# Samples' attention over the cache: two samples at a time, queries as weights, value products on 32-column strips

## The reference

```python
def _nsa_sel_attend(q, qpos, idx, kvb):
    ...
    s = jnp.einsum('btgrd,btgkld->btgrkl', q, kb) * dh ** -0.5
    kpos = idx[..., None] * NSA_BLOCK + jnp.arange(NSA_BLOCK)
    mask = kpos <= qpos[None, :, None, None, None]
    p = _masked_softmax(s.reshape(B, T, G, R, -1), mask.reshape(B, T, G, 1, -1))
    return jnp.einsum('btgrn,btgnd->btgrd', p, vb.reshape(B, T, G, -1, dh).astype(jnp.float32))
...
    o = gt[..., 0:1] * o_c + gt[..., 1:2] * o_s + gt[..., 2:3] * o_w
```

## Time and profile before

| | us |
|---|---|
| median of 3 runs | 4247.26 (4228.52 to 4252.52) |
| the profiled execution, its own time | 4233.27 |
| its span in the trace | 4231.4 |
| mean granted clock of PE, share of full speed | 0.897 |
| the samples' units, from about 1880 to 2396 in the span | 516 |

### The profile page before, as it was taken

The page is one execution under the profiler, slowest core; times in us unless marked ns, Lnnn a source line. Parts: engine busy times, 40 slices in busy tenths (PEclk is TensorE's granted clock), DMA queues, the critical chain, the costliest instruction groups (busy, mean ns, idle before and its releaser), DMA issues. The chain is left out here.

```text
span 4231.4 us, 44095 instructions
## 1 busy us (share of the span) xinstructions
PE 3769.7 (89%) x17890; PEld 2507.1 (59%) x17890; DVE 1431.0 (34%) x3327; ACT 546.9 (13%) x1219; POOL 181.7 (4%) x279
## 2 busy tenths in 40 slices
PE   7998989999999999869888457676879999999998
PEld 4665666665677776658776443333446556665676
DVE  3445322233132232265564346542242213211111
ACT  1000011000111001111121024441011000100000
POOL 3111100000000000000000000000000000000000
PEclk8999999999999999866666658888999999999999
DMA  6565542322343323351221320004003333233443
GB/s 162 172 189 162 171 120 81 86 61 85 115 118 88 98 82 108 105 111 48 72 92 65 73 85 8 6 3 157 15 10 116 89 96 112 74 90 95 138 122 96
DMA packets 601110, 399.64 MB, mean 94 GB/s; under 512 B 90140, under 2 KB 577933, under 8 KB 596429
## 3 DMA queue, kind: packets, MB, share of 16 engines
q1 hardware_dynamic: 573084, 312.00, 27.1%
q0 software_dynamic: 13824, 67.12, 4.6%
q10 hardware_dynamic: 14000, 17.71, 1.2%
HBM read 364.80 MB, written 36.13 MB: 95 GB/s over the span
## 5 line engine op out<-in xcount | busy, mean ns | idle before, releaser
L400 PE MATMUL psum<-arena 128*128 128x384 f32 (+1 forms) x4224 | 1338.0, 475 | 24.3 <-DVE arena L535 15.8
L400 PEld LDWEIGHTS psum<-arena 128*128 128x128 f32 x4224 | 799.8, 192 | 493.2 <-issue 32.3
L410 PE MATMUL psum<-arena 128*128 128x384 f32 (+1 forms) x2112 | 662.1, 472 | 0.0
L410 PEld LDWEIGHTS psum<-arena 128*128 128x128 f32 x2112 | 399.9, 191 | 235.4 <-issue 4.8
L433 PE MATMUL psum<-arena 128*128 128x384 f32 (+3 forms) x816 | 271.4, 489 | 0.0
L549 DVE SCALAR_TENSOR_TENSOR arena<-arena,psum 128x384 f32<-128x384 f32 (+1 forms) x132 | 70.3, 532 | 582.0 <-ACT arena L487 581.8
L487 ACT ACTIVATE arena<-psum 128x384 f32<-128x384 f32 (+1 forms) x132 | 62.5, 473 | 1356.6 <-PE psum L400 1356.6
L565 DVE SCALAR_TENSOR_TENSOR arena<-psum,arena 128x384 f32<-128x384 f32 (+1 forms) x96 | 51.4, 536 | 506.6 <-PE psum L410 506.6
L558 DVE TENSOR_TENSOR arena<-psum,arena 128x384 f32<-128x384 f32 (+1 forms) x132 | 70.7, 536 | 423.0 <-PE psum L400 422.1
L433 PEld LDWEIGHTS psum<-arena 128*128 128x128 f32 (+1 forms) x816 | 153.2, 192 | 96.3 <-issue 19.5
L3406 PE MATMUL psum<-arena 128*128 128x128 f32 x528 | 87.6, 318 | 86.5 <-DVE arena L3503 54.1
(11 more groups left out here) (582 smaller groups left out, 3655.0 us busy)
## 6 DMA issues: line engine op xcount, KB each, us to landing
arena<-in_ffa_up SPq DMA_DIRECT2D x132, 512.0 KB, 5.2
arena<-in_ffb_up SPq DMA_DIRECT2D x132, 512.0 KB, 5.2
arena<-in_ffa_down SPq DMA_DIRECT2D x48, 704.0 KB, 4.5
arena<-in_ffb_down SPq DMA_DIRECT2D x48, 704.0 KB, 4.5
arena<-in_w_in SPq DMA_DIRECT2D x27, 1024.0 KB, 5.8
arena<-in_w_in SPq DMA_DIRECT2D x9, 1056.0 KB, 6.0
pT<-arena ACTq DMA_DIRECT2D x32, 192.0 KB, 5.3
arena<-xs SPq DMA_DIRECT2D x2, 2176.0 KB, 14.9
```

The source lines that it names most:

```text
L400: ins = mm(b[:, 0:n], w[:, g, k], hC[:, k, 0:n], start=(k == 0), stop=(k == KD - 1))
L410: ins = mm(b[:, 0:n], w[:, k], actT[:, k, 0:n], start=(k == 0), stop=(k == FH - 1))
```

## The change

Two samples are worked on together: sample 2u+x lies on partitions 64x to 64x+63 of everything that has queries on partitions. There are 4 pairs u, each with 4 page units c = 0 to 3 (one page of 1024 rows from each sample) and the window unit c = 4, 20 units v in all, one every 2 rounds: 46 rounds instead of 53.

- Scores: the 64 query columns are now the weights and 512 turned keys the moving side; two samples write to column strips 0 to 63 and 64 to 127 of one bank. A page unit has two such pairs (`scores(v, 0)`, `scores(v, 1)`), a window unit one. Scores lie with queries on partitions and cached rows along the free side.
- DVE adds the mask, scales and takes the running minimum in one instruction (`tensor_tensor_reduce`, in `masked`), ACT's exponential has that minimum as bias and gives the sum (`accum_out`). The turns of the maximum, the spreading and the matmul of sums go away. The exponentials of a pair's four page units are brought to one maximum at its end.
- The weights must be turned (`turn_weights`, 8 for a page unit) and copied by ACT (`weights`) before the value products.
- Value products: one for each sample, tile of 128 rows and group: 32 weight columns, 64 value columns, written to strip 64x+32g. There are 576 of these where there were 288 of 64 by 128.
- The window rows go to free places of `sVB`, loaded by SP when a unit is done. Gathers for unit v+3 start when unit v's values of the same x are read. The compressed branch is laid out by pairs as well. 16 small loads of gate biases move to ACT's queue.

The core of the diff (left out: the layout of tiles, the small loads, the masks' preparation, and the finish of a pair, `6 in stage` and `7 in stage`, with about 15 small DVE operations for each u):

```diff
         SA_FIRST = 10
-        SA_UNITS = sorted([(SA_FIRST + 6 * q + 3 * h, 0, q, h) for q in range(NB) for h in range(2)] +
-                          [(SA_FIRST + 6 * q + 1, 1, q, 0) for q in range(NB)])
-        SA_ROUNDS = SA_FIRST + 6 * NB - 3 + 8
+        SA_UNITS = [(u, c) for u in range(4) for c in range(5)]
+        SA_ROUNDS = SA_FIRST + 2 * len(SA_UNITS) + 6
 
         def sa_active(r):
 
-            return [(br, q, h, r - start) for start, br, q, h in SA_UNITS if 0 <= r - start <= (5 if br else 6 + h)]
+            units = [(v, r - SA_FIRST - 2 * v) for v in range(len(SA_UNITS))]
+            return [(v, s) for v, s in units if 0 <= s <= (7 if SA_UNITS[v][1] == 4 else 5)]
...
@@ sa_pe
+            def keys(v, x):
+                u, c = SA_UNITS[v]
+                if c == 4:
+                    pe.wait_ge(cache_in[x], 16 * (u + 1))
+                else:
+                    pe.wait_ge(sa_pages[sa_slot(v, x)], sa_gathered(v, x))
+                for half in range(1 if c == 4 else 2):
+                    b = bank(rt)
+                    for t in range(4):
+                        ins = turn(b[:, t * P:(t + 1) * P], sVB[sa_slot(v, x)][:, 4 * half + t, 0:P], ident)
+                    ins.then_inc(rt.full, 1)
+                turned[v] = rt.n
+
+            def scores(v, half):
+                u, c = SA_UNITS[v]
+                pe.wait_ge(rt.read, turned[v])
+                b = bank(rs)
+                for x in range(2):
+                    ins = mm(b[64 * x:64 * x + 64], QB[:, 2 * u + x], sKT[2 * x + half], start=True, stop=True, skip_group_check=True)
+                ins.then_inc(rs.full, 1)
+
+            def new_scores(v):
+                u, c = SA_UNITS[v]
+                b = bank(rv)
+                for x in range(2):
+                    ins = mm(b[64 * x:64 * x + 64, 0:64], QB[:, 2 * u + x], KTn[:, 1 if c == 4 else 0], start=True, stop=True, skip_group_check=True)
+                ins.then_inc(rv.full, 1)
+
+            def turn_weights(v):
+                u, c = SA_UNITS[v]
+                pe.wait_ge(scalar_for_tensor, pe.due(scalar_for_tensor))
+                n = 4 if c == 4 else 8
+                for half in range(n // 4):
+                    b = bank(rt)
+                    for t in range(4):
+                        j = (4 * half + t) * P
+                        ins = turn(b[:, t * P:(t + 1) * P], saS[:, j:j + P], ident)
+                    ins.then_inc(rt.full, 1)
+                if c >= 3:
+                    turn(bank(rt)[0:64, 0:P], saS[:, n * P:n * P + 64], ident).then_inc(rt.full, 1)
+                turned[v] = rt.n
+
+            def values(v, x):
+                u, c = SA_UNITS[v]
+                pe.wait_ge(rt.read, turned[v])
+                o = bank(rv)
+                n = 4 if c == 4 else 8
+                p = [slice(64 * x + 32 * g, 64 * x + 32 * g + 32) for g in range(2)]
+                for t in range(n):
+                    for g in range(2):
+                        ins = mm(o[p[g], 0:64], saPT[:, t, p[g]], sVB[sa_slot(v, x)][:, t, P + 64 * g:P + 64 * g + 64],
+                                 start=(t == 0), stop=(t == n - 1 and c < 3), skip_group_check=True)
+                if c >= 3:
+                    for g in range(2):
+                        j = (640 if c == 4 else 384) + 64 * g
+                        ins = mm(o[p[g], 0:64], saPT[0:64, 8, p[g]], NRs[:, j:j + 64], start=False, stop=True, skip_group_check=True)
+                ins.then_inc(rv.full, 1)
...
-            def turned(br):
-                from_vector()
-                turn(bank(rv)[0:64, 0:P], sX[:, br], ident).then_inc(rv.full, 1)
-
-            def spread_out(br):
-                from_vector()
-                mm(bank(rv)[:, 0:64], sREP[:, br], ident[0:64, 0:64], start=True, stop=True).then_inc(rv.full, 1)
-
-            def values(br, q, h):
-                pe.wait_ge(scalar_for_tensor, pe.due(scalar_for_tensor))
-                o = bank(rv)[0:64, 0:P]
-                tiles = [(sSTw[:, t], sVBw[:, t]) for t in range(4)] if br else \
-                    [(sST[:, h, t], sVB[(4 * q + 2 * h + t // 8) % 6][:, t % 8]) for t in range(16)]
-                new = br or h
-                for t, (p, v) in enumerate(tiles):
-                    ins = mm(o, p, v[:, P:2 * P], start=(t == 0), stop=(t == len(tiles) - 1 and not new), skip_group_check=True)
-                if new:
-                    c = 640 if br else 384
-                    ins = mm(o, sNW[:, br], NRs[:, c:c + P], start=False, stop=True, skip_group_check=True)
-                ins.then_inc(rv.full, 1)
...
+                stage = {s: v for v, s in sa_active(r)}
+                if 2 in stage:
+                    scores(stage[2], 0)
+                if 4 in stage:
+                    values(stage[4], 0)
+                if 5 in stage:
+                    values(stage[5], 1)
+                if 2 in stage:
+                    if SA_UNITS[stage[2]][1] < 4:
+                        scores(stage[2], 1)
+                    if SA_UNITS[stage[2]][1] >= 3:
+                        new_scores(stage[2])
+                if 3 in stage:
+                    turn_weights(stage[3])
+                if 0 in stage:
+                    keys(stage[0], 0)
+                if 1 in stage:
+                    keys(stage[1], 1)
...
@@ sa_act
+                if 3 in stage:
+                    weights(stage[3])
+                if 0 in stage:
+                    keys(stage[0], 0)
+                if 1 in stage:
+                    keys(stage[1], 1)
+                if 2 in stage:
+                    u, c = SA_UNITS[stage[2]]
+                    n = (4 if c == 4 else 8) * P + (64 if c >= 3 else 0)
+                    w = saW[:, u % 2, c]
+                    act.wait_ge(vector_for_scalar, act.due(vector_for_scalar))
+                    done(a.activation(saS[:, 0:n], saS[:, 0:n], ACT.Exp, bias=w[:, 0:1], scale=-1.0, accum_out=w[:, 1:2]))
+                    act.eng.sem_inc(scalar_for_tensor, act.one(scalar_for_tensor))
...
@@ sa_dve
+            def masked(b, v, at, n, mask, first, ring):
+                u, c = SA_UNITS[v]
+                w = saW[:, u % 2, c, 0:1]
+                read(e.tensor_tensor_reduce(out=saS[:, at:at + n], in0=b[:, 0:n], in1=mask, scale=negs[:, 0:1],
+                                            scalar=(3e38 if first else w), op0=ALU.add, op1=ALU.min, accum_out=w), ring)
+
+            def taken(v, x):
+                u, c = SA_UNITS[v]
+                p = slice(64 * x, 64 * x + 64)
+                read(e.tensor_copy(SOU[p, u % 2, c], full(rv)[p, 0:64]), rv)
...
+                if 2 in stage:
+                    v = stage[2]
+                    masked(full(rs), v, 0, 512, WINM if SA_UNITS[v][1] == 4 else SELM, True, rs)
+                if 4 in stage:
+                    taken(stage[4], 0)
+                if 5 in stage:
+                    taken(stage[5], 1)
+                if 1 in stage and SA_UNITS[stage[1]][1] == 0:
+                    weights_mask(stage[1])
+                if 2 in stage:
+                    v = stage[2]
+                    u, c = SA_UNITS[v]
+                    if c < 4:
+                        masked(full(rs), v, 512, 512, SELM, False, rs)
+                    if c >= 3:
+                        masked(full(rv), v, 512 if c == 4 else 1024, 64, NEWM[:, u], False, rv)
+                    to(vector_for_scalar)
```

455 lines of the change are left out of this document (181 added, 274 removed).

## The result

| | median of the runs, us | ratio to before |
|---|---|---|
| before | 4238.22 (4228.52 to 4252.52) | |
| changed | 4048.07 (4044.95 to 4048.98) | 0.9547 [0.9513, 0.9582] |

The profiled execution took 4047.79 us (before 4233.27), with a span of 4046.1 (before 4231.4). The span is 185 us shorter, where the sum had 106. One run each of two kernels further down, before_wide (5648 us) and before_fill (4904 us), was slow, at a granted clock of 0.63 and 0.75 over the whole kernel: the medians there count it and move by 0.2 us or less, the ratios leave it out.

A forecast was written before the change was run, and what follows sets the result against it. The prediction took the units (516.2 us) as bound by PE's work at a low clock, plus waits. Savings of 52 (work), 14 (idle) and 40 (clock), 106 us, gave 4127, plus 5 for the median: 4132 us, range 4070 to 4195.

The forecast's parts named there:

- less PE work at the old clock: Units: scores 41 and maximum and sum 29.5 saved, turns of weights 36 added, values 17 saved: 52 us less.
- idle: PE's waits in the units: 34 us before the maximum's and sum's matmuls go, 20 come: 14 us less.
- clock: PE's clock in the units: fast half of the time instead of a third, so 396 us become 356, 40 less.
- Values: Value products in the units: 1216 records at 0.053, 65 us, plus 8 for group ends: 73 against 89.9, 17 saved.
- (1): Idle: `scores(v, 1)` waits for DVE's reading of `scores(v, 0)`, 0.7 us on 20 rounds: 14 us.
- (2): Idle: turned weights and keys follow each other, 16 turns waiting on ACT's four copies: 4 us.
- (3): Idle: the exponential must end before the next round's turns of weights: 2 us added.
- Preparation and transfers: Before and beside the units: DVE's first operation 4 us later but hidden, gathers two rounds ahead; net 0.
- C: Rival: clock at 0.85 and values costing 44 us, 165 us saved, 4073; chance 0.12.
- B: Rival: the clock doesn't move, since column strips use part of the array; 66 us saved, 4172; chance 0.14.
- D: Rival: waits (1) to (3) all uncovered, 67 us instead of 20, clock stays; 19 saved, 4219; chance 0.06.
- E: Rival: every change of strip paid like a change of shape, values 213 us; 74 us slower, 4312; chance 0.06.

The follow-up runs named there:

- before_wide: Kernel before, with score products moving 128 columns (two samples' queries) instead of 64: 4216.48 us, ratio 0.9944.
- before_fill: Kernel before, with one useless matmul of 512 moving columns ahead of each of 24 waits for the maximum: 4233.67 us, ratio 0.9974.
- before_nomax: Kernel before without the maximum: its turn, spreading and subtraction left out: 4148.76 us, ratio 0.9776.
- before_wide_nomax: Kernel before with scores moving 128 columns and the maximum left out, both at once: 4129.63 us, ratio 0.9733.
- values_grouped: Changed kernel, value products ordered all of one key-value head, then the other, so neighbours write the same strip: 4062.28 us, ratio 0.9571.
- scores_in_four: Changed kernel, every score product of 512 columns cut into four of 128, strips in turn: 4050.82 us, ratio 0.9544.
- scores_one_strip2: Changed kernel, both samples' score products on strip 0 from the second unit on: 4073.66 us, ratio 0.9615.
- masks_twice: Changed kernel, each masking of scores on DVE made twice: 4066.55 us, ratio 0.9575.
- values_four: Changed kernel, value products of both samples in one round and one bank, four strips of 32 in turn: 4044.17 us, ratio 0.9546.
- four_keys_first: values_four with the second sample's key turns and copies moved ahead of the weights' turns and copies in odd rounds: 4041.63 us, ratio 0.9529.
- values_four_stream: values_four with one useless matmul of 448 columns ahead of each unit's value products, 20 in all: 4074.84 us, ratio 0.9604.
- fill_ends: Changed kernel, with 36 useless matmuls of 384 columns on PE at the start of the stage behind the samples' attention: 4051.14 us, ratio 0.9561.

## Why the prediction failed, step by step

**The yardstick.** The lanes' work in the units is the same in both kernels, so it shows how much quicker work went. Before it is the 447.8 us less the 287.0 of the earlier trace rows and less four small groups of the samples, 9.1 us, which the forecast had counted with the lanes:

```profile
L2697 PE MATMUL psum<-arena 64*128 64x64 f32 x8 | 2.8, 354 | 0.0
L2710 PE MATMUL psum<-arena 128*64 128x64 f32 x16 | 2.6, 246 | 0.0
L2703 PE MATMUL psum<-arena 128*64 128x64 f32 x16 | 2.6, 246 | 0.0
...
L2723 PE MATMUL psum<-arena 64*64 64x64 f32 x8 | 1.1, 311 | 2.9 <-DVEq L2817 2.9
```

That leaves 151.7. After it is 289.6 less the groups of the samples (45.4, 43.7, 42.7, 22.7, 5.0, 2.7, 2.4, and 2.0 and 1.1 of L2643 and L2729), 121.9. So the same work went 151.7 / 121.9 = 1.24 times as quickly. The forecast's own rule says the same: a clock of 0.86 is 72% of the time fast, (1 + 0.8 x 0.72) / 1.26 = 1.25. I take 1.25. Then PE's 289.6 us would have been 362 at the mean clock of before.

| term | forecast, us | measured, us |
|---|---|---|
| less PE work at the old clock | 52 | 448 - 362 = 86 |
| idle | 14 | 68.4 - 43.6 = 25 |
| clock | 40 | 362 - 290 = 72 |
| sum | 106 | 183 |

**The clock: the step that failed.** "I take half of the time fast instead of a third": it was 72% of the time, nearly the bound that I gave as "three quarters fast". The term is 72 us instead of 40, and it is more than that. The forecast also took one mean clock for all work, and the turns of keys, which the change leaves alone, went 67.7 / 43.7 = 1.55 times as quickly. At the mean they would have gone from 67.7 to 54; the other 10 us of their gain, 13 at the old clock, stand in the table as work. With them the clock is 85 us where 40 were forecast, 45 of the 77 us missed. The direction was right, and both causes that the step names hold: the columns of the scores, and the waits for the maximum with what goes together with them, each lift the clock to about 0.75, together to 0.82 (before_wide, before_nomax, before_wide_nomax). What was wrong was to take a middle value although the timeline showed both causes go at once. It is also where the waits cost more than their 33.8 us: the same work took 34 us more in before than in before_nomax. The last step from 0.82 to 0.86 was not separated, and it is hardly more than two profiles of the same code differ by.

The work term was the second miss, 86 us instead of 52: 13 of its 34 are the turns of keys, 10 the values, 5 each the scores and the turns of weights, and 2 the new tokens' scores, which I had left out on both sides. The idle time was 11 us better than forecast.

**Values.** Forecast were 65 us for the records and 8 for the ends of the groups, 73. Measured are 50.4 us, at the old clock 50.4 x 1.25 = 63. So the price was right (0.034 and 0.060 us a record, where the row of the lane work had 0.036 and 0.062), and only the 8 us for ends don't exist. The question beside it, whether strips run side by side with all 128 rows in use, is answered by values_grouped: they do, and the lane work's row had it in it because it changes place at each matmul too. The Trainium skill says so (TensorEngine Tiling (Array Packing), Key Properties): tiles operate independently and can load weights and multiply in parallel. I had weighed only the point ahead of that one in its list, on the drain. The trace agrees with the second point: 1.78, 1.09 and 0.55 us for 32 records on one, two and four strips. No time shows for a change between strips of one shape, and no run here tests a change of shape. (The forecast counted 5 of those in a unit. By its own orders there are 7, if strips of 64 and of 32 are told apart; it put none of them into its sum.)

**Turns of keys.** I left them at 67.7 us, as work that the change doesn't touch. A turn took 0.235 us before, nearly the slow price of 0.246, and 0.152 after, nearer to the fast 0.136: by these prices an estimated tenth of them ran fast before and 85% after. In before_nomax they fall to 56.0 while the clock of the units is 0.75. The forecast priced scores and lane work at either clock, but not a turn, so it didn't see that the turns stood below the mean.

**Scores and turns of weights.** The forecast of 58.6 us for scores is 42.7 x 1.25 = 53 for the pairs: a pair took 1.19 us, near the fast price of 1.08. The turns of weights were put at 36, by the slow price of the turns of keys, and are 25.1 x 1.25 = 31. Both sizes held within 5 us. Columns set the price of the scores, as scores_in_four shows, and running on two strips nearly halves it (scores_one_strip2).

**Maximum and sum.** Their matmuls are gone, as forecast.

**Idle.** 33.8 us went, and 9 net came back, not 20. (1) The wait of `scores(v, 1)` for the masking is 6.1 us, not 14. It is on the edge, though: masks_twice, 0.7 us more for each masking, costs 18 us. (2) The copies of weights hold up the turns of keys by 7.1 us (4 forecast). (3) The exponential holds up the turns of weights by 1.9 us (2 forecast).

**Preparation and transfers.** Forecast 0. DVE's step at L1978 starts at 1815.7 (before 1814.7), behind the same wait for the state. No matmul of the changed kernel's units waits for a gather.

**The rivals.** C came closest, with a clock of 0.85, but neither its 44 us for values (63 at the old clock) nor the waits that it held against itself came. B is refuted by the clock, D by an idle time that fell, E by the strips in turn.

## What to carry to other kernels

Where the granted clock is low, a wait can cost more than its idle time: look at the price of the matmuls right behind it, and add what they would save at the fast clock. Don't give all work one mean clock: a group whose price is the slow one, as here the turns of keys, has more to gain than the mean. Read the clock's effect from work that the change leaves alone, here the lanes (1.24 times) and the turns of keys (1.55 times), and take every group of the changed part out of it first. Small products on several column strips should take the strips in turn, neighbour by neighbour. But once other waits stand beside PE's work (here at values_four), the same trick again moves the time by 4 us for 23 us of work, and the wait for ACT's exponential grows from 1.9 to 10.2 us.

## What was not expected of the hardware

- Products of 32 weight columns and 64 moving columns took 1.78 us for 32 records on one strip, 1.09 on two in turn and 0.55 on four.
- The clock is not told by PE's busy share. It was 0.67 at 87% busy in before, 0.86 at 83% in masks_twice and 0.79 at 87% in four_keys_first. Useless columns lifted it in before_fill (0.67 to 0.75) and not in values_four_stream (0.84 and 0.82; over the whole kernel 0.919 to 0.922 in the runs of values_four and 0.916 to 0.918 in its own). The same code of the units had 0.85, 0.86 and 0.88 in three executions, so the 0.88 and 0.89 of scores_one_strip2 and values_grouped, where the same products kept PE busy longer, are not shown to be more. What sets it in such a mix stays open.
- The clock was not spread evenly over the groups. The same turns of keys went 1.55 times as quickly in the changed kernel (0.235 us and then 0.152 each), the lanes 1.24 times.
- In fill_ends the clock that the fillers had gained, 0.69 from 2250 to 2270, was back at 0.50 in the next 30 us, although PE was busy for 24.4 of them.
